# A two-block transformer kernel: the order of squares, sums, weight rounding and waits at the ends of ten stages is changed

## The reference, cut to what matters

```
x = x + 0.5 * swiglu(rms_norm(x, ffn_norm[l, 0]), w_gate, w_up, w_down)
p = rms_norm(x, mix_norm[l]) @ w_in[l]
def rms_norm(x, g, eps=NORM_EPS):
    y = xf * lax.rsqrt(jnp.mean(xf * xf, axis=-1, keepdims=True) + eps)
    return y * g
```

## Time and profile before

| what | us |
|---|---|
| median of 3 runs | 3878.84 |
| lowest and highest | 3876.53, 3888.51 |
| the profiled execution's own time | 3880.47 |
| its span, first to last instruction | 3878.7 |
| TensorE busy in it | 3616.8 (93%) |
| mean granted clock of TensorE | 0.947 of full |

### The profile page before, as it was taken

How to read it: one execution, slowest core, us unless ns; L and a number is a source line. 1 busy time by engine, 2 the same in 40 slices (tenths; PEclk the granted TensorE clock), 3 DMA queues, 4 the chain that set the end, 5 groups by cost and what they waited for, 6 DMA issues and landing times.

```text
span 3878.7 us, 46821 instructions
## 1 busy us (share of the span) xinstructions
PE 3616.8 (93%) x17424; PEld 2973.0 (77%) x17424; DVE 1634.5 (42%) x2716; ACT 1236.3 (32%) x1849; POOL 1233.9 (32%) x516
## 2 busy tenths in 40 slices
PE   7999997689999999999778999988899999889999
PEld 6888775577888888877567788867677888777887
DVE  5440596755331433158575533122455221323220
ACT  3222435223222322243532322232233332323331
POOL 3444330004444444433000444423101444323443
PEclk9999997799999999999779999988899999999999
DMA  4442220003442344222000344222001222112222
GB/s 168 145 146 98 71 85 3 1 1 122 143 144 105 131 144 143 98 71 76 6 1 1 125 144 143 103 71 71 28 6 44 98 97 98 65 60 81 97 98 92
DMA packets 93532, 332.04 MB, mean 86 GB/s; under 512 B 10432, under 2 KB 12128, under 8 KB 93280
## 3 DMA queue, kind: packets, MB, share of 16 engines
q1 hardware_dynamic: 77136, 274.65, 20.2%
q10 hardware_dynamic: 16272, 55.65, 4.1%
HBM read 327.64 MB, written 2.62 MB: 85 GB/s over the span
## 4 chain that ended last, share of the span: by engine, by line
PE 83%; DVE 10%; ACT 2%; issue 2%; DMA 2%; SPq 0%; DVEq 0%; ACTq 0%
PE ps L1806 21%; PE ps L1808 21%; PE ps L1807 21%; DMA w_raw<-in_tiles 2%; PE ps L1825 1%; PE ps L2546 1%; PE ps L1826 1%; PE ps L1830 1%; DVE sq L1091 1%; PE ps L1950 1%; PE ps L1843 1%; PE ps L2102 1%; PE ps L2531 1%; DVE mem L1248 1%; DVE stat L1247 1%
## 5 line engine op out<-in xcount | busy, mean ns | idle before, releaser
L457 POOL TENSOR_TENSOR w_lo<-w_raw,w_hi 128x1024 fp32r<-128x1024 f32 x512 | 1233.7, 2411 | 2621.2 <-ACT w_hi L479 2621.0
L1806 PE MATMUL ps<-h_hi,w_hi 128*128 128x512 f32 x2656 | 1045.2, 394 | 13.6 <-DVE mem L1693 7.9
L1808 PE MATMUL ps<-h_hi,w_lo 128*128 128x512 f32 x2656 | 1035.4, 390 | 0.0
L1807 PE MATMUL ps<-h_lo,w_hi 128*128 128x512 f32 x2656 | 1035.0, 390 | 0.0
L479 ACT ACTIVATE w_hi<-w_raw 128x1024 fp32r<-128x1024 f32 x512 | 541.6, 1058 | 1076.1 <-DMA w_raw<-in_tiles 1075.9
L1806 PEld LDWEIGHTS ps<-h_hi,w_hi 128*128 128x128 f32 x2656 | 499.6, 188 | 134.0 <-issue 19.3
L1807 PEld LDWEIGHTS ps<-h_lo,w_hi 128*128 128x128 f32 x2656 | 499.8, 188 | 106.1 <-issue 3.4
L1808 PEld LDWEIGHTS ps<-h_hi,w_lo 128*128 128x128 f32 x2656 | 499.3, 188 | 104.4
L1153 DVE TENSOR_TENSOR a_lo<-sil,a_hi 128x512 f32 (+1 forms) x132 | 296.7, 2248 | 485.2 <-ACT a_hi L616 485.2
L1806 PE MATMUL ps<-a_hi,w_hi 128*128 (+1 forms) x1056 | 410.8, 389 | 0.0
L1807 PE MATMUL ps<-a_lo,w_hi 128*128 (+1 forms) x1056 | 410.8, 389 | 0.0
(11 more groups left out here) (445 smaller groups left out, 4017.9 us busy)
## 6 DMA issues: line engine op xcount, KB each, us to landing
w_raw<-in_tiles SPq DMA_DIRECT2D x512, 512.0 KB, 3.2
ada_raw<-in_ada_tiles ACTq DMA_DIRECT2D x96, 512.0 KB, 3.2
x<-in_x_t SPq DMA_DIRECT2D x2, 1024.0 KB, 6.4
sq<-in_cond ACTq DMA_DIRECT2D x4, 512.0 KB, 4.1
out_t<-x SPq DMA_DIRECT2D x1, 2048.0 KB, 7.1
consts<-in_consts SPq DMA_DIRECT2D x1, 1280.0 KB, 12.7
mem<-in_ctx_t ACTq DMA_DIRECT2D x1, 1024.0 KB, 6.7
core_mem<-in_consts ACTq DMA_DIRECT2D x1, 576.0 KB, 3.8
```

Source lines behind the costliest of these rows:

```text
L457: nc.gpsimd.tensor_tensor(w_lo[:, s, :], w_raw[:, s, :], w_hi[:, s, :].bitcast(F32), ALU.subtract).then_inc(S["w_lo_ready"], 1)
L1806: nc.tensor.matmul(bank, wh, hi, start=first, stop=False, skip_group_check=True)
L1807: nc.tensor.matmul(bank, wh, lo, start=False, stop=False, skip_group_check=True)
L1808: return nc.tensor.matmul(bank, wl, hi, start=False, stop=last, skip_group_check=True)
```

## The change: what it does

- In `round_out` (four output projections) ScalarE squares chunk k, and makes its raw high half where there is one, ahead of rounding tile k + 4. VectorE adds the square of chunk k in the same turn as the update of chunk k, not one turn later.
- At the end of a feed-forward ScalarE rounds one tile less ahead of the last four squares; that tile joins `late_tiles`, which then holds two.
- The first half of the sums (the 8 matmuls over square_sum) becomes `sum_first`. After an output projection it is issued inside the last tile, behind the seventh of its eight blocks, and `sum_squares` then has only the 8 matmuls over the last square.
- The raw pair always uses banks 4 and 5; after mix_out it waits for seven updates of x in place of three. The next pair of tiles in a raw feed-forward waits for one activation less, and `first_tiles` behind the raw pair has no such wait.
- ScalarE's h_hi no longer waits for the raw pair's matmuls where the raw halves lie in a_lo.
- The table of the root is loaded through a scratch column `unused`, with a wait for its own end; `load_silu` does the same for Silu after the late tiles of a feed-forward that begins with a raw pair.

```
--- before.py
+++ after.py
@@ -134,6 +134,7 @@
 
             return squares[(n - 1) % len(squares)] if n else square_sum
         rtok = sb("rtok", [P, TB])
+        unused = sb("unused", [P, 1])
         head_tok = sb("head_tok", [P, 96])
         ada = sb("ada", [P, 2, ADA_TILES])
         gmod = sb("gmod", [P, 2, KD])
@@ -314,7 +315,7 @@
 
         def raw_banks(name):
 
-            return (4, 5) if RAW[name].startswith("ffn") else (0, 1)
+            return 4, 5
 
 
         def raw_order(name):
@@ -494,7 +495,11 @@
 
             def load_sqrt():
 
-                nc.scalar.activation(rtok[:, 0:1], eps(EPS_ONE), ACT.Sqrt)
+                link(nc.scalar.activation(unused[:, :], eps(EPS_ONE), ACT.Sqrt))
+
+            def load_silu():
+
+                link(nc.scalar.activation(unused[:, :], eps(EPS_ONE), ACT.Silu))
 
             def raise_raw(name, k):
 
@@ -506,22 +511,24 @@
                 early, todo = seen.pop("early"), order[seen.pop("raw_early"):]
                 for n in range(early, KD):
                     square_x(n, order[n], updates)
-                    if early + 2 == KD:
-                        raise_raw(name, todo[n - early])
-                if early + 2 < KD:
-                    for k in todo:
-                        raise_raw(name, k)
+                for k in todo:
+                    raise_raw(name, k)
                 act.wait_ge(S["ss_ready"], due("norms"))
                 nc.scalar.activation(rtok[:, :], ps[:, 7, 0:TB], ACT.Sqrt, scale=1.0 / D, bias=eps(EPS_NORM)).then_inc(S["std_ready"], 1)
                 for t in seen.pop("late_tiles"):
                     round_tile(t)
                 if name.startswith("ffn") and int(name[-1]) < 4:
                     load_cond(int(name[-1]))
+                if name.startswith("ffn"):
+                    load_silu()
+                in_place = RAW[name].startswith("ffn")
                 for n, k in enumerate(order):
                     act.wait_ge(S["hf_ready"], due("hf_ready"))
                     if n < KD - 1:
-                        act.wait_ge(S["raw_used"], due("raw_used"))
-                    else:
+                        used = due("raw_used")
+                        if in_place:
+                            act.wait_ge(S["raw_used"], used)
+                    elif in_place:
                         act.wait_ge(S["w_used"], base + 2)
                     nc.scalar.activation(h_hi[:, k, :], sil[:, n % 2, :], ACT.Copy).then_inc(S["h_hi_ready"], 1)
                     if n in (4, KD - 1):
@@ -547,13 +554,12 @@
 
                 load_sqrt()
                 for k in range(KD - 1):
+                    square_x(k, k, updates + 1)
+                    if after:
+                        raise_raw(after, k)
                     round_tile(base + k + 4)
-                    if k:
-                        square_x(k - 1, k - 1, updates + 1)
-                        if after:
-                            raise_raw(after, k - 1)
-                seen["raw_early"] = KD - 2
-                seen["early"] = KD - 2
+                seen["raw_early"] = KD - 1
+                seen["early"] = KD - 1
                 seen["late_tiles"] = [base + KD - 1 + 4]
 
             def round_h(chunks, shift=None):
@@ -643,9 +649,9 @@
                         for c in range(KD // 2):
                             raise_raw(after, FFN_ORDER[c])
                     seen["early"] = seen["raw_early"] = KD // 2
-                for t in range(down + 13, down + NF - 1):
+                for t in range(down + 13, down + NF - 2):
                     round_tile(t + 4)
-                seen["late_tiles"] = [down + NF - 1 + 4]
+                seen["late_tiles"] = [down + NF - 2 + 4, down + NF - 1 + 4]
 
             act.wait_ge(S["basics_loaded"], 48)
             seen["late_tiles"] = range(2, RING)
@@ -1632,10 +1638,10 @@
                 for k in range(KD):
                     dve.wait_ge(S["w_used"], base + k + 1)
                     V.tensor_tensor(x[:, k, :], x[:, k, :], ps[:, (k - 1) % KD, :], ALU.add).then_inc(S["x_ready"], 1)
-                    add_square(max(k - 1, 0))
-                    if 0 < k < KD - 1:
-                        lower_raw(RAW_NEXT[f"mix_out{l}"], k - 1)
-                seen["raw_early"] = KD - 2
+                    if k < KD - 1:
+                        add_square(k)
+                        lower_raw(RAW_NEXT[f"mix_out{l}"], k)
+                seen["raw_early"] = KD - 1
 
 
             def modulate(layer, part, gain, which=0, slot=0):
@@ -1807,11 +1814,13 @@
                 nc.tensor.matmul(bank, wh, lo, start=False, stop=False, skip_group_check=True)
                 return nc.tensor.matmul(bank, wl, hi, start=False, stop=last, skip_group_check=True)
 
-            def linear_tile(bank, t, i=None, step=RING):
+            def linear_tile(bank, t, i=None, step=RING, between=None):
 
                 pe.wait_ge(S["w_lo_ready"], t + 1 if i is None else step * i + (t + 1))
                 for k in range(KD):
                     ins = products(bank, t % RING, k * P, h_hi[:, k, :], h_lo[:, k, :], k == 0, k == KD - 1)
+                    if between and k == KD - 2:
+                        between()
                 ins.then_inc(S["w_used"], 1)
 
             def first_tiles(t, banks=(0, 1), order=range(KD)):
@@ -1833,16 +1842,20 @@
 
             def sum_squares():
 
-                norms = due("norms")
-                for last, chunk in enumerate((square_sum, square_slot(KD - 1))):
-                    if last:
-                        pe.wait_ge(S["sq_ready"], KD * norms)
-                    else:
-                        pe.wait_ge(S["sq_added"], (KD - 2) * norms)
-                    for j in range(TB):
-                        ins = nc.tensor.matmul(ps[:, 7, j:j + 1], chunk[:, j * P:(j + 1) * P], const("ones", 0, 1),
-                                               start=(last == 0 and j == 0), stop=(last == 1), skip_group_check=True)
+                if not seen.pop("sum_begun", 0):
+                    sum_first()
+                pe.wait_ge(S["sq_ready"], KD * seen["norms"])
+                for j in range(TB):
+                    ins = nc.tensor.matmul(ps[:, 7, j:j + 1], square_slot(KD - 1)[:, j * P:(j + 1) * P], const("ones", 0, 1),
+                                           start=False, stop=True, skip_group_check=True)
                 ins.then_inc(S["ss_ready"], 1)
+
+            def sum_first():
+
+                pe.wait_ge(S["sq_added"], (KD - 2) * due("norms"))
+                for j in range(TB):
+                    nc.tensor.matmul(ps[:, 7, j:j + 1], square_sum[:, j * P:(j + 1) * P], const("ones", 0, 1),
+                                     start=(j == 0), stop=False, skip_group_check=True)
 
             def norm_sums():
 
@@ -1860,7 +1873,7 @@
 
                 updaters = [n for n in run if n.startswith("ffn") or n.endswith("_out") or "mix_out" in n]
                 banks = raw_banks(name)
-                pe.wait_ge(S["x_ready"], KD * updaters.index(RAW[name]) + 3)
+                pe.wait_ge(S["x_ready"], KD * updaters.index(RAW[name]) + (3 if RAW[name].startswith("ffn") else KD - 1))
                 (hi, lo), t, order = raw_parts(name), BASE[name], raw_order(name)
                 sums_at = 3 if RAW[name].startswith("ffn") else 1
                 first = seen.get("raw_chunk", 0)
@@ -1891,21 +1904,22 @@
                 if not raw:
                     norm_sums()
 
-                def up_pair(i, j):
-
-                    pe.wait_ge(S["af_ready"], NF * n + 2 * i + (j + 1))
+                def up_pair(i, j, late=0):
+
+                    pe.wait_ge(S["af_ready"], NF * n + 2 * i + (j + 1 - late))
                     linear_tile(ps[:, 2 * j, :], base + 2 * j, i)
                     linear_tile(ps[:, 2 * j + 1, :], base + 2 * j + 1, i)
 
                 pe.wait_ge(S["af_ready"], NF * n + 1)
                 if raw:
                     raw_tiles(name)
-                    pe.wait_ge(S["af_ready"], NF * n + 2)
                     first_tiles(base + 2, (2, 3), raw_order(name))
+                    up_pair(1, 0, 1)
+                    up_pair(1, 1)
                 else:
                     first_tiles(base)
                     up_pair(0, 1)
-                with pe.Fori(1, NF // 2) as i:
+                with pe.Fori(1 + int(raw), NF // 2) as i:
                     for j in range(2):
                         up_pair(i, j)
                 down = base + 2 * NF
@@ -2384,7 +2398,8 @@
 
                 first_tiles(base, (7, 0), order)
                 for k in range(2, KD):
-                    linear_tile(ps[:, k - 1, :], base + k)
+                    linear_tile(ps[:, k - 1, :], base + k, between=sum_first if k == KD - 1 else None)
+                seen["sum_begun"] = 1
 
 
             def linear_ctx(bank, t):
```

## The result

The changed kernel takes **3924.9 us** (median of 4 runs, 3920.02 to 3924.98) beside 3883.68 us for the kernel before in the same session (4 runs, 3876.53 to 3891.39): ratio 1.0103, 95% interval 1.0078 to 1.0127. It is slower by 1%, outside the predicted range. Its profiled execution took 3924.97 us with a span of 3923.2.

A forecast was written before the change was run, and what follows sets the result against it. TensorE was taken to bound the kernel, busy 3616.8 of 3878.7 us. Terms of 12.6, 11.1, 6.5, 4.0, 2.8 and 3.8 summed to 40.8 us, less 3 gave 38: median forecast 3841, range 3829 to 3861.

The forecast's parts named there:

- Step 7: Table loads: `load_silu` moves a 1.28 us load from before the first Silu to the spread's time; counted 0.
- The one on the slower side: Sums break into the last tile, the clock falls earlier and stays low longer; 3886 with 7 us more each; chance 0.04.
- The list of what would show the prediction wrong: TensorE waiting where it didn't, in the last tile above all, or clock rows looking as before.
- Feed-forward ends, idle: Squares before the tile: idle before sums goes at three raw transitions (5.3 us); 3.0 gained after ffn3, 3.2 after ffn4.
- Projections, idle: Squares before the tile after output projections: idle 0.25 for 2.46 us with a raw pair, 1.65 for 3.21 without.
- Half of the sums inside the last tile: After the four output projections, 8 of 16 sums run at full clock: 0.7 to 0.9 us gained in each.
- Clock: Stays high over most raw transitions, 12.6 us for three and 11.1 for two with idle; falls later at the other four.
- The 3 us taken off for two falls: Deduction from the 40.8 us sum for two raw transitions where the clock still falls, 1.5 us each.
- the first rival: Clock falls as often as before, the one-column sums alone keeping it low; gain 24 us, so 3855; chance 0.24.
- the third: Rival: clock never falls at a transition; gain 54 us, so 3825; chance 0.06.
- One more late tile: Two GpSimd subtractions in a row hold VectorE's first h_lo: costs 1.6 us in the Fourier stage, 0.6 in mla_in.
- Looser waits: The three waits at the third pair of tiles of ffn1, ffn2 and ffn3 go: 3.8 us gained.

## Why the prediction was wrong

**The step that failed** is an allocation that the prediction never priced. Step 7 gave the two table loads, "Counted 0", and spoke of the time of a table load; the column that they write to is in the diff and in no term, as if memory that does nothing costs nothing. It costs 85.5 us, by slowing matmuls that the change doesn't touch. No rival held it either. The one on the slower side (sums that break into the last tile) had the right sign and a mechanism that did not happen. The list of what would show the prediction wrong looked at waits and at clock rows, both of which came out as forecast, and not at the duration of an untouched matmul, which alone gave the cause away.

**What the rest of it was worth** is read with the tensors in place. The forecast of 3841 stands against 3839.4 and 3841.5. That it is met to 2 us is partly luck: the kernel before had other medians in those sessions (3885.5 and 3883.0, where the forecast started from 3878.8), so the gain was 46 and 42 us where 38 were forecast. The spans differ by 43.2 us (3878.7 and 3835.5); the terms made 40.8, and 38 once 3 were taken off for the clock.

The traces bear the sum out part by part. From the end of the last tile to the first matmul behind the spread, with 0.8 us added where half of the sums stands inside the tile, the nine transitions took 93.6 us before and take 55.7: 37.9 less, where their terms made 37.0. The three after a raw feed-forward gave 12.7 (12.6 counted), the two after mix_out 11.5 (11.1), mla_out and fourier_out 6.1 (6.5), ffn3 4.7 (4.0), ffn4 2.9 (2.8). In the changed kernel as it stood they take 54.4. So what the prediction reasoned about came true in the very kernel that was slower.

1. *Feed-forward ends, idle.* Right. No wait before the sums at the three raw transitions, 1.38 and 1.44 us at the two others, where 1.4 and 1.5 were counted. Adds take 0.68 us, not 2.48. VectorE, ffn0 to att_in0, in the changed kernel with the column in rtok's slot:

```profile
387.84 0.68 DVE L1097 TENSOR_TENSOR sq<-sq 128x512 f32<-128x512 f32 x1
388.59 0.69 DVE L1188 SCALAR_TENSOR_TENSOR x<-ps,x 128x512 f32<-128x512 f32 x1
389.20 0.68 DVE L1097 TENSOR_TENSOR sq<-sq,sil 128x512 f32<-128x512 f32 x1
```

2. *Projections, idle.* Right. Counted 0.25 and 1.65; there was 0.05 after mix_out0 and mix_out1, and 1.50 after mla_out and fourier_out.

3. *Half of the sums inside the last tile.* The place is as forecast (L1857 stands inside the tile without a wait), the gain isn't: step 3 gave 0.7 to 0.9 us to each of four (the sum has 0.9 for each of the two without a raw pair and books the other two under the clock), and taking it out cost nothing. After mix_out the reason for a gain, half clock during the sums, was gone by step 2; after the other two the sums behind the tile would have filled idle time. TensorE, mla_out to ffn4, same kernel:

```profile
2948.88 0.94 PE L1857 MATMUL ps<-consts,sq 128*128 128x1 f32 x8
...
2952.14 1.87 PE L1849 MATMUL ps<-consts,sq 128*128 128x1 f32 x8 [1.50 <-ACT sq L494]
2954.64 2.08 PE L1869 MATMUL ps<-consts,rtok 128*128 128x128 f32 x8 [0.63 <-DVE rtok L1114]
```

Here the clock did fall, and the second half ran at the low level, where the prediction counted both halves at the high one. After fourier_out they did run so, 1.05 us for the second half.

4. *Clock.* Right, and better than taken: it stays high in all five raw transitions (each takes 4.0 us, counted as above) and falls at the four others. Windows of ffn0 to att_in0, mix_out0 to ffn1 and mla_out to ffn4, same kernel:

```profile
392.40:397.10 4.70, 4.70 (x35) 4.30 (x34) 2.81 (x6) 3.52 (x6) 1.46 (x1) 1.00 0.08 30
905.50:908.90 3.40, 3.34 (x24) 3.07 (x24) 0.93 (x2) 2.27 (x5) 0.25 (x1) 1.00 0.46 158
...
2951.90:2960.00 8.10, 5.54 (x20) 4.90 (x21) 3.25 (x6) 2.91 (x6) 2.34 (x1) 0.51 0.18 62
```

The 3 us taken off for two falls were not needed. The first two rows refute the first rival, in which the clock falls as often as before, the last one the third, in which it never falls. One reading of the prediction goes with them: from the 3.48 busy of 3.50 us at half clock it took it that idleness isn't needed. Ahead of that window lie 1.84 us of idle; with none, the same sixteen sums kept 1.00. The Trainium skill's rule ("TensorE: Matmul & The Clock Gate", Part 1 on the clock gate) is that the clock drops when TensorE has been idle. The trace agrees at all nine: 1.4 to 1.5 us of idle at the four that fell, none over 0.06 us at the five that didn't. What the prediction made of it was wrong: it put "never falls" beside the rule, while by its own steps 1 and 2 four transitions would still have 1.4 to 1.65 us of idle.

5. *One more late tile.* Mechanism right, 1.6 counted and 2.05 measured: the Fourier stage waits 5.97 in place of 3.92 us. In mla_in the first six matmuls take 3.24 us from start to start, where they took 2.69: 0.55 more, and 0.6 were counted. In the Fourier stage the first h_lo takes 2.81 us beside two subtractions on GpSimd (VectorE, then GpSimd, then TensorE):

```profile
3326.76 2.81 DVE L1084 SCALAR_TENSOR_TENSOR h_lo<-sil,ada,h_hi 128x512 fp32r<-128x512 f32 x1
```

```profile
3324.28 4.74 POOL L458 TENSOR_TENSOR w_lo<-w_raw,w_hi 128x1024 fp32r<-128x1024 f32 x2 [8.76 <-ACT w_hi L480]
```

```profile
3331.16 0.77 PE L2591 MATMUL ps<-w_hi,h_hi 128*128 128x512 f32 x1 [5.97 <-DVE h_lo L1084]
```

h_lo ends at 3329.57, 0.55 us after GpSimd is through at 3329.02, where it takes 0.75 us undisturbed. That fits the Trainium skill ("SBUF — State Buffer", section "SBUF: two separate sides"), by which a VectorE operation with two operands in SBUF and a reading GpSimd operation shut each other out for a whole instruction.

6. *Looser waits.* The 3.8 us are gained, but there were two cures for them. With the old wait put back (and `load_silu` kept) only 0.58 us return. The traces show why: from VectorE's first product of the raw pair to the end of its third (L1145 to L1148, L1151 to L1154 in the changed kernel) 4.14 us passed before and 2.86 pass now at each of the three places, 1.28 less. That is the table load of the earlier trace rows, and it is as long as each of the three waits was, 1.25 to 1.26 us; 0.58 is left in ffn2, where TensorE also comes to the pair sooner than before. So step 7's "Counted 0" for `load_silu` is right only beside step 6; by itself it would have brought most of the 3.8. The reverse, the looser wait without `load_silu`, was not run.

When the feed-forward ends were put back as they had been, the stretches that end in the five transitions grew by 19.8 us, where the terms of these five were 12.6 + 4.0 + 2.8 = 19.4.

## To carry to other kernels

Where an edit adds or drops an allocation, compare the operands' addresses as part of the diff, and put small scratch tensors ahead of all operands of the matmuls or inside an existing slot: a column that no instruction named cost 1.7%. After a change, look first at the count of an untouched instruction in a window in which its engine never stops; if that moved at the same granted clock, look for the cause outside the schedule. And if a wait and a low clock have one cause, don't price two cures for it: the second one found nothing left (the sums inside the tile, and the looser wait beside the table load).

## What the hardware showed

- With 128x512 fp32r matmuls back to back at granted clock 1.00, the pitch depends on where the operands lie to each other: 226.7 to 227.3 ns where w_hi, w_lo and the moving operand lie a multiple of 256 bytes apart and are moved in steps of 32 bytes; 230.0 where both are moved by 16; 233.1 to 233.3 with 32 bytes between them; 228.8 to 229.2 with the moving side 64 bytes on. Over the kernel that is 3839, 3925 and 3871 us. With 256 or 128 columns the 32 bytes cost at most 1.1 ns. What in the chip does it was not found out, nor whether other types do the same.
- The Trainium skill ("TensorE: Matmul & The Clock Gate", section "Wait — 56ns, not 53.3ns?") gives the interval as a matter of the column count alone, 215.7 ns at 512 columns. Here no row has it: the fastest is 226.7, with a weight load before each matmul, and it is not constant.
- Sixteen one-column sums between full matmuls don't bring the clock down by themselves: 1.00, where the stretch had 0.52 with 1.84 us of idle ahead of it.
